# Hybrid NSA/MLA decode layer on one core: decode transposes, rope rows, input scalings, last gate half and last output rows put in another order

## The reference

```python
def _mla_attend(q_lat, q_pe, t, c, kr, pos_k):
    s = (jnp.einsum('bqhc,bsc->bhqs', q_lat, c) + jnp.einsum('bqhr,bsr->bhqs', q_pe, kr)) * MLA_SCALE
    mask = (pos_k[None, :] <= t[:, None])[None, None]
    p = _masked_softmax(s, mask)
    return jnp.einsum('bhqs,bsc->bqhc', p.astype(c.dtype), c)
...
def _merge_out(x, o_a, o_lat, gates, w_kv_up, w_proj_a, w_proj_b, w_out, norm_post):
    ga, gb, ma, mb = gates
    b, t = x.shape[:2]
    o_b = jnp.einsum('bqhc,chv->bqhv', o_lat, w_kv_up[..., MLA_NOPE:]).reshape(b, t, MLA_WIDTH)
    pa = (o_a * jax.nn.silu(ga)) @ w_proj_a
    pb = (o_b * jax.nn.silu(gb)) @ w_proj_b
    h = jax.nn.sigmoid(ma) * pa + jax.nn.sigmoid(mb) * pb
    return x + _rmsnorm(h @ w_out, norm_post)
```

## Time and profile before

| | |
|---|---|
| median of 3 runs | 675.36 us (674.79 to 683.52) |
| the profiled execution | 675.11 us |
| its span, first to last instruction | 673.3 us |
| PE busy | 651.5 us, 97% of the span |
| DVE busy | 447.4 us, 66% |
| ACT busy | 214.8 us, 32% |
| POOL busy | 79.5 us, 12% |
| mean granted TensorE clock | 0.995 |

### The profile page before, as it was taken

The page is one execution under the profiler, slowest core; times in us unless marked ns, Lnnn a source line. Parts: engine busy times, 40 slices in busy tenths (PEclk is TensorE's granted clock), DMA queues, the critical chain, the costliest instruction groups (busy, mean ns, idle before and its releaser), DMA issues.

```text
span 673.3 us, 15352 instructions
## 1 busy us (share of the span) xinstructions
PE 651.5 (97%) x5771; PEld 433.0 (64%) x5771; DVE 447.4 (66%) x1232; ACT 214.8 (32%) x586; POOL 79.5 (12%) x91
## 2 busy tenths in 40 slices
PE   9999999999999998899999998999999999999994
PEld 3444444553576765667777675678788888886442
DVE  2198899686577777766665663637585757649864
ACT  0311321776444454444443532421011111110221
POOL 0344343125000000120211000000000000000011
PEclk9999999999999999999999999999999999999997
DMA  8999999999989999978759789975411111027011
GB/s 337 417 422 424 424 427 400 361 369 283 344 296 378 398 395 413 374 245 316 273 179 361 230 276 403 407 280 219 157 63 63 63 63 63 1 109 300 2 63 62
DMA packets 67587, 179.44 MB, mean 267 GB/s; under 512 B 7513, under 2 KB 16498, under 8 KB 60218
## 3 DMA queue, kind: packets, MB, share of 16 engines
q1 hardware_dynamic: 56088, 125.14, 50.9%
q0 software_dynamic: 8640, 48.90, 17.9%
q10 hardware_dynamic: 2786, 4.42, 1.8%
HBM read 169.38 MB, written 12.72 MB: 270 GB/s over the span
## 4 chain that ended last, share of the span: by engine, by line
PE 88%; DVE 5%; issue 2%; ACT 2%; SPq 1%; DMA 1%; DVEq 0%; another core or an unknown queue 0%; ACTq 0%
PE bank L1554 20%; PE bank L973 12%; PE bank L1393 8%; PE bank L1605 7%; PE bank L1254 5%; PE bank L958 4%; PE bank L1377 4%; PE bank L1362 3%; PE bank L1280 3%; PE bank L1264 3%; PE bank L1583 2%; PE bank L1137 2%; PE bank L1327 2%; PE bank L1337 1%; PE bank L1408 1%
## 5 line engine op out<-in xcount | busy, mean ns | idle before, releaser
L973 PE MATMUL bank<-W,XG 128*128 128x494 f32 x192 | 83.5, 579 | 0.0
L1862 ACT ACTIVATE projP<-bank,projP 128x128 f32<-128x128 f32 (+3 forms) x96 | 49.8, 523 | 41.8 <-DVE projP L2341 41.5
L2641 DVE TENSOR_TENSOR projP<-projP,bank 128x260 f32<-128x260 f32 x81 | 32.6, 423 | 42.3 <-PE bank L1554 41.6
L1654 ACT ACTIVATE projP<-bank 128x128 f32<-128x128 f32 (+5 forms) x87 | 33.7, 391 | 84.0 <-PE bank L1554 47.7
L1393 PE MATMUL bank<-W 128*128 128x260 f32 x256 | 60.4, 389 | 0.0
L973 PEld LDWEIGHTS bank<-W,XG 128*128 128x128 f32 x192 | 35.2, 192 | 35.6 <-issue 35.0
L1393 PEld LDWEIGHTS bank<-W 128*128 128x128 f32 x256 | 47.3, 190 | 10.8 <-issue 3.7
L2341 DVE CUSTOM_DVE_ANT_0 bank<-bank,maskb 128x128 f32<-128x128 f32 (+3 forms) x96 | 45.8, 511 | 12.0 <-PE bank L1254 10.6
L1654 ACT ACTIVATE W<-bank 128x512 f32<-128x512 f32 (+2 forms) x69 | 40.1, 582 | 38.7 <-PE bank L1016 11.6
L809 POOL DMA_INDIRECT ring<-cmp,idxi x32 | 38.6, 1207 | 67.5 <-DVE VV L2052 47.7
L1254 PE MATMUL bank<-W 64*128 64x128 f32 (+7 forms) x192 | 46.0, 466 | 0.5 <-ACT projP L1862 0.4
(11 more groups left out here) (477 smaller groups left out, 1165.7 us busy)
## 6 DMA issues: line engine op xcount, KB each, us to landing
ring<-latent SPq DMA_DIRECT2D x168, 256.0 KB
XG<-latent SPq DMA_DIRECT2D x56, 256.0 KB
W<-w_gate SPq DMA_DIRECT2D x12, 1024.0 KB, 4.7
W<-w_attn SPq DMA_DIRECT2D x16, 494.0 KB, 11.7
W<-latent SPq DMA_DIRECT2D x20, 256.0 KB, 4.9
rope_rows<-ring SPq DMA_DIRECT2D x16, 256.0 KB, 7.0
KRR<-rope_rows ACTq DMA_DIRECT2D x16, 256.0 KB
ring<-win SPq DMA_DIRECT2D x8, 512.0 KB
```

Source lines behind the costliest of these rows:

```text
L973: mm = pe.matmul(bank[2 * (u % 2) + n][:, 0:GW], XG[:, k * TOK + tl * P:k * TOK + (tl + 1) * P], w_part(half, k, n), start=(k == 0), stop= ...
L1654: return act.activation(dst, src, ACT.Copy, scale=scale)
L1862: act.activation(Pb[u % 4][:, 0:w], bank[u % 2][:, 0:w], ACT.Exp, bias=NMp[:, u:u + 1], scale=-1.0, accum_out=RSp[:, u:u + 1]).then_inc(S[ ...
L2641: dve.tensor_tensor(out, a, pair_bank(v, product)[:, 0:HALF], ALU.add).then_inc(S["z_by_dve"], 1)
```

## The change

It alters the order of instructions and the place of two kinds of data; no arithmetic is added or left out.

- **Decode transposes.** All chunks from step 16 on use bank 7 (`TURN_IN_7`). The five `K_at` steps stay in step `d`+1 but change bank, and no longer wait for the copy of the last key block. The chunks of steps 17, 20, 22, 42 and 44 move from the end of step `d` to behind the scores of step `d`+1.
- **Input scalings.** One of the three `scale_input` of each of steps 20 to 24, and the one of step 25, moves ahead of the first `scale_p` of its step.
- **Group 26.** Two of its homes change; its first four pages are issued ahead of groups 22 to 24, with a wait for unit 64 instead of 80.
- **Rotary rows.** Pairs 13 and 15 get a home of their own, in `PTd`. Pair 13's load is issued right behind pair 12's, and the later ones one pair earlier than before.
- **Gate half of step 48.** On PE it moves behind the transposes of the step; its tanh and silu move into step 49.
- **Last rows.** The two quarters of the last half's product with the norm weights move from POOL to DVE, and the second quarter's sum moves ahead of an `out_half`.
- The store of the window state counts on the semaphore of the output rows.

```diff
-                 J_LATE: [W[:, at:at + 512] for at in (0, 512, 1024, 2048, 8256, 8768, 9280, 9792)]}
+                 J_LATE: [W[:, at:at + 512] for at in (0, 512, 2048, 3072, 8256, 8768, 9280, 9792)]}
+        ROPE_APART = (13, 15)
+
+        def rope_home(p2):
+            return PTd[:, :] if p2 in ROPE_APART else KRR[:, 0:512]
...
-        TURN_FIRST = {d for d in SOFT_at if d >= 16 and d not in K_at}
-        X2_FIRST, X2_PER = 20, 3
+        TURN_IN_7 = {d for d in SOFT_at if d >= 16}
+        TURN_FIRST = {d for d in TURN_IN_7 if d not in K_at and d not in (17, 20, 22, 42, 44)}
+        X2_PIECES = {20: range(0, 3), 21: range(3, 6), 22: range(6, 9), 23: range(9, 12), 24: range(12, 15), 25: range(15, 16)}
...
+            sp.wait_ge(S["s"], 64)
+            latents(26, 0, 4)
             for m in range(22, 25):
                 latents(m)
             sp.wait_ge(S["ds"], max(c["q"] for c in chunks if c["kind"] == "slc") + 1)
-            sp.wait_ge(S["s"], 80)
-            latents(26)
+            latents(26, 4, 8)
...
                 if keys_before(d + 1):
-                    pe.wait_ge(S["keys_by_A"], 3 * keys_before(d + 1) - (d in K_at and d in TURN_FIRST))
-                if d in TURN_FIRST:
+                    pe.wait_ge(S["keys_by_A"], 3 * keys_before(d + 1) - (d in K_at and d in TURN_IN_7))
+                if d in TURN_IN_7:
                     pe.wait_ge(S["do"], c["q"])
...
-                if d in G_at:
+                if d in G_at and d != PAIRS:
                     gate_half(d)
...
                 if d in TURN_FIRST:
                     dec_transposes(d)
+                if d == PAIRS:
+                    gate_half(d)
...
-                    if c["kind"] == "mla" and c["no"] < 15:
-                        load_rope(c["no"] + 1)
-                if d in G_at:
+                    if c["kind"] == "mla" and c["no"] < 14:
+                        load_rope(c["no"] + (1 if c["no"] < 12 else 2))
+                    if c["kind"] == "mla" and c["no"] == 11:
+                        load_rope(13)
+                if d == PAIRS + 1:
+                    gate_tanh(G_at[PAIRS])
+                if d in G_at and d != PAIRS:
                     gate_tanh(G_at[d])
...
+                for i in X2_PIECES.get(d, ())[:1]:
+                    scale_input(i)
                 if d < PAIRS:
                     scale_p(2 * d)
...
             root_of(1, 1)
+            dve.wait_ge(S["z_by_dve"], out_added["c21a", 1])
+            last_normed(0)
             dve.wait_ge(S["sqz"], SQUARES.index((3, 0, "a")) + 1)
             dve.tensor_tensor(vfirst[:, 3:4], vfirst[:, 3:4], ssz[:, 10:11], ALU.add).then_inc(S["mean_sq"], 1)
+            rows_added("c21", 1, rows(3, 0), rows(3, 0), "p4", 256, 512)
             out_half(1, 0)
-            rows_added("c21", 1, rows(3, 0), rows(3, 0), "p4", 256, 512)
+            dve.wait_ge(S["z_by_dve"], out_added["c21", 1])
+            last_normed(256)
             out_half(1, 1)
             root_of(3, 0)
             out_half(3, 0)
```

44 lines of the change are left out of this document (24 added, 20 removed).

## The result

The changed kernel takes 666.10 us (median of four runs, 665.36 to 667.52) against 675.08 before: 0.986 of it, with an interval of 0.982 to 0.990. On a second chip, with five runs of the one and nine of the other, it was 665.02 against 675.37, 0.985 (0.983 to 0.986). It is 9 to 10 us faster. I had forecast 671.3 and a range down to 668.8, so the direction was right, the gain that I forecast (4.1) was less than half of the measured one, and the time lies outside the range.

The account below looks back on a forecast made before the run. PE was taken to bound the kernel, busy 651.5 of 673.3 us, so only its loop waits could shrink. The terms summed to 4.09 won off 675.11, giving 671.0 profiled and 671.3 for the median, range 668.8 to 675.0.

Parts of the forecast that it names:

- Bank of the five transposes: Steps 17, 25, 29, 33, 37: transposes slip ahead of the wait for ACT's key copy; 0.95 us won, bounds 0 and 1.4.
- Chunks of steps 17, 20 and 22: Decode transposes moved behind the next step's scores: 0.25, 0 and 0.56 us won, with a new wait of 0.55 in step 18.
- Scaling of step 23: One scaling moved to where DVE waits for ACT, so its copy comes sooner; 0.43 us won, bounds 0 and 0.68.
- Gate half of step 48: Gate matmuls placed between transposes and outputs cover the late copy; 0.68 us won, bounds 0 and 0.68.
- Chunk of step 44: Transposes moved behind the scores, which then wait only for exponentials; 0.48 us won, bounds 0 and 0.53.
- Page group 25 and chunk of step 42: Page wait of 0.83 us goes, exponentials are next late; 0.74 us won, bounds 0.3 and 1.14.
- The wait of 1.4 with no releaser I leave as it is.: Unlabelled PE wait ahead of L1377 in step 43, read as PE waiting for its code; assumed unchanged.
- by whatever it is: Rival that more comes free: the unlabelled 1.4 us wait goes too, giving 669.9; chance 0.15 for 667 to 669.9.
- The last rows: Program end: DVE's added products are offset by time regained beside POOL; 0 won, bounds 0.5 won and 0.5 lost.
- The floor of 666.8: Time if every listed wait of PE in the loop went, 8.5 us won.
- Slower by 2%: Whole kernel 2% (13.5 us) slower, said to take nine more waits for code; chance 0.01.

Follow-up runs that it names:

- before_again: The kernel before, unchanged, run again for a second profile; the two profiles of that kernel are at 675 and 676 us.
- bank_only: The kernel before with only the bank of the five decode transposes behind key steps changed, nothing moved; 674.31 us in a single run.
- x2_gate48: The kernel before with only the scalings' edit (steps 20 to 25) and the gate half of step 48; 673.18 us in a single run.
- before_edge120: The kernel before with its two warm-up matmuls of 512 columns cut into 32 thin ones, 120 PE instructions more; 684.23 us, 1.014.
- no_pages: The changed kernel with the page groups as before, the four pages of group 26 not early; 669.51 us, 0.9904 of the time before.
- before_shift: The kernel before with 32 tiny matmuls more at the start of PE's program, 128 instructions in the trace; 685.1 us in one run.
- pages_only: The kernel before with only the page groups' edits, four pages of group 26 early; 672.99 us in a single run.
- turns_only: The kernel before with all the decode transposes' edits alone, both bank and moved chunks; 672.87 us, 0.9964.
- rope_only: The kernel before with only the rotary rows' edits for pairs 13 and 15; 674.74 us in a single run.
- tail_only: The kernel before with only the last rows' edit, two quarter products moved from GpSimd to VectorE; 673.34 us, 0.9958.

## Why the prediction was wrong, point by point

Measured against before_again, whose profile is free of the long wait in step 22. What PE has won by the outputs of step 49 is 6.66 + 0.36 = 7.0, the end gives 2.15, together 9.2.

- *Bank of the five transposes*, 0.95 forecast, upper bound 1.4: 1.36 (bank_only). The place was right, size and reason were off. Steps 25 and 33 gave 0.40 and 0.42 over before_again where I had put 0.25: not the transposes' own length was won but nearly the whole wait (0.47 and 0.56 there), and the scores behind them stood at most 0.05.
- *Chunks of steps 17, 20 and 22*, 0.25 + 0 + 0.56 = 0.81: 0.35 + 0.04 + 0.54 = 0.93. The new wait ahead of the value product in step 18 is there, 0.38 for my 0.55, marked "issue" but ending 0.1 behind ACT's copy. The wait at step 21 is 0.99, at the top of what I had said.
- *Scaling of step 23*, 0.43: 0.41 (x2_gate48, step 24), right in mechanism and size. The scaling of step 22, for which I had put nothing because DVE has no gap there, gave 0.34 more, by way of the exponentials and not of DVE's copy.
- *Gate half of step 48*, 0.68: 0.79 in the changed kernel from step 45 to 49, where before_again lost 0.25 (partly a page wait of 0.18); 0.76 in x2_gate48. *Chunk of step 44*, 0.48: 0.54.
- *Page group 25 and chunk of step 42*, 0.74 with bounds of 0.3 and 1.14. This step failed. Taking the page edit out of the changed kernel costs 4.4 (6.66 - 2.27). The prediction capped its worth at the waits that stood in one trace. In the profile of before the wait for group 25 was 0.83; it was 0.98 in before_again, behind a stop in step 41, 1.5 in before_edge120, 1.93 in no_pages, 2.0 in bank_only, 2.2 in before_shift. SP let group 26 out from 392.54 in the first profile and 392.15 in the second, 7.41 ahead of the outputs of step 41 in both, and the scores of step 42 started 15.6 and 16.7 behind it. So I had taken the low end of something that varies by execution for its size. But the wait for the page makes only 0.5 of the 4.4, which lies inside my bounds. The rest is the code stop (1.98) and the clock (1.7), neither of which I had given to this edit: the term counted the page alone, and not who else stands behind the same loads. It was not that gains upstream come back here: SP's issue is tied to PE's progress and moves along.
- *"The wait of 1.4 with no releaser I leave as it is."* This step failed too. That it was PE waiting for its code fits all the runs; that the change would leave it alone was not right, since the page edit takes load out of just that stretch (286 and 301 GB/s against 395 and 405 from 402 to 406, in pages_only and before, both on the clock of before). It was absent in all seven profiles with the page edit, half or whole, and no shift, pages_only among them, and it stood, at 1.43 to 1.98, in no_pages, turns_only, bank_only, rope_only, tail_only and both profiles of before. I had it as a rival with a chance of 0.15, "by whatever it is", without seeing that one of the edits was a cause for it. As to the rule of the Trainium skill that I weighed there (Runtime: NRT & Kernel Launch, Instruction fetch mechanics: crossing to the next block is mostly hidden): "mostly" holds, as at most two of the 46 packets of a profile left an unlabelled wait of over 0.2 behind, but 1.4 to 2.0 us stood open where the loads filled the DMA engines, so the conclusion I drew from it, that the gap would be no fetch, does not.
- *The last rows*, 0 with bounds of 0.5 either way: 2.15. This step failed by what it looked at. The reckoning on DVE was right (its last row moved 0.15 against PE's end), but the question was what ends the program. I followed the last `out_half` and its store and took everything behind it as fixed. The list of closing instructions showed GpSimd's DRAIN from 665.5 to 673.1 in the profile of before.
- The floor of 666.8 was worked out as the sum of PE's waits in the loop. The time came out below it, since 2.15 of the gain is not in PE's waits at all. The sum was also short: the list it was taken from has the 1.1 ahead of L1337 and 0.4 ahead of L1254, which were left out, and its 2.7 hold 0.46 of step 8, which the change doesn't touch.
- *Slower by 2%* was said to take nine more waits for code. It takes over 12, as the 4.1 won have to be lost first: (13.5 + 4.1) / 1.43.

The sum now: 1.36 + 0.93 + 0.75 by step 41, that is 3.04, and 4.04 - 0.99 = 3.05 in the changed kernel. From 41 to 44 it has won 1.3 where before_again lost 1.1: 2.4, as much as the page wait (0.98) and the code stop (1.43) of before_again. 0.54 and 0.79 + 0.25 behind that: 7.0. And 2.15: 9.2, of the 9.0 and 10.35 by the medians.

What stays open: nothing in x2_gate48 touches the loads or PE's code ahead of step 43, and yet its packet went out 1.1 behind PE's number 8410, with 370 GB/s around it, while in tail_only 379 GB/s went with 8.2. So that full DMA engines delay the packet is argued from agreement, and no run changed the loads of this stretch without touching the pages. It is not shown either which part of the page edit is needed, the pages sent early or the wait for unit 80 that went. Nor is it known what GpSimd does in the 6.5 us of its drain.

## What to carry to other kernels

Look at which transfers an edit takes out of a full stretch, and who else stands in that queue: here an edit to the page loads was worth six times the 0.74 that I charged it with, by the code and the clock that came with it. Read what ends the program from the closing instructions of every engine, not from the last row of work: in this kernel two small products of GpSimd, the last of them begun 5.5 us before SP had seen the last store (665.5 and 671.0), cost 2.15 us. And take two profiles of the kernel before: a stop of PE or a page's lateness by 1 us can stand in one and not in the other.
